# A hybrid decoder layer on one core: the first norm's factor is applied to the results instead of to x

## What is computed

```python
h = rmsnorm(x, norm1[l])           # x * rsqrt(mean(x*x) + EPS) * norm1, per token
z = h @ w_in[l]                    # D = 1024 channels in
(z_rx, z_ry, z_q, z_kc, z_vc, z_ks, z_vs, z_kw, z_vw, z_ng, z_mg) = ...
xr = rg_lru(causal_conv(z_rx, conv_w, conv_b), ...)
y_a = (xr * gelu(z_ry)) @ w_rg_out
q  = rmsnorm(z_q per head, q_norm);  k_s, k_w = rmsnorm(z_ks), rmsnorm(z_kw) per head
kc = rmsnorm(compress(z_kc, ...));   vc = compress(z_vc, ...)   # pos added, 2 layers, gelu
y_b = nsa(q, kc, vc, k_s, z_vs, k_w, z_vw, sigmoid(z_ng)) @ w_nsa_out
x = x + (sigmoid(z_mg)[0] * y_a + sigmoid(z_mg)[1] * y_b) @ w_o
# then the second norm and the SwiGLU block, which the change leaves alone
```

## Time and profile before

| what | value |
|---|---|
| time, median of 3 runs | 483.1 us (482.95 to 483.11) |
| the profiled execution | 483.16 us |
| its span, first to last instruction | 481.4 us |
| granted TensorE clock | 1.000 |
| busy: TensorE, VectorE, ScalarE, POOL | 475.2, 354.7, 280.3, 16.3 us |
| read from HBM | 83.22 MB, 175 GB/s over the span |

### The profile page before, as it was taken

How to read it: one execution, slowest core, us unless ns; L and a number is a source line. 1 busy time by engine, 2 the same in 40 slices (tenths; PEclk the granted TensorE clock), 3 DMA queues, 4 the chain that set the end, 5 groups by cost and what they waited for, 6 DMA issues and landing times.

```text
span 481.4 us, 7336 instructions
## 1 busy us (share of the span) xinstructions
PE 475.2 (99%) x2795; PEld 410.0 (85%) x2795; DVE 354.7 (74%) x630; ACT 280.3 (58%) x451; POOL 16.3 (3%) x27
## 2 busy tenths in 40 slices
PE   7999999999999999999999999999999999999997
PEld 7998998788999777877788888888888888888886
DVE  3999899699897886766754758777777777764332
ACT  4755886775777897566753435755555555453320
POOL 2000210220000000000000000000000000000000
PEclk9999999999999999999999999999999999999999
DMA  8755979724243346243434452655555455555402
GB/s 309 264 170 195 372 290 257 274 88 175 88 144 120 135 159 231 91 174 95 167 116 147 150 205 83 247 197 199 208 199 176 176 181 191 207 208 175 174 1 87
DMA packets 12993, 85.78 MB, mean 178 GB/s; under 512 B 1568, under 2 KB 1824, under 8 KB 3104
## 3 DMA queue, kind: packets, MB, share of 16 engines
q1 hardware_dynamic: 12096, 82.32, 47.5%
q0 software_dynamic: 432, 2.10, 1.5%
q10 hardware_dynamic: 432, 0.91, 0.5%
HBM read 83.22 MB, written 1.05 MB: 175 GB/s over the span
## 4 chain that ended last, share of the span: by engine, by line
PE 98%; DVE 0%; POOL 0%; issue 0%; ACT 0%; POOLq 0%; DVEq 0%
PE bank L1121 19%; PE bank L1122 19%; PE bank L1123 19%; PE bank L1159 16%; PE bank L1162 8%; PE bank L1295 3%; PE bank L1242 2%; PE bank L1331 2%; PE bank L1535 1%; PE bank L1304 1%; PE bank L1252 1%; PE bank L1379 1%; PE bank L1314 1%; PE bank L1338 1%; PE bank L1335 1%; PE bank L1279 0%
## 5 line engine op out<-in xcount | busy, mean ns | idle before, releaser
L680 DVE TENSOR_TENSOR w_lo<-raw,w_hi 128x2048 fp32r<-128x2048 f32 x71 | 162.5, 2290 | 49.9 <-ACT w_hi L375 49.6
L375 ACT ACTIVATE w_hi<-raw 128x2048 fp32r<-128x2048 f32 x72 | 138.0, 1917 | 48.0 <-PE bank L1123 41.4
L1159 PE MATMUL bank<-h_hl,w_hi 128*128 128x512 f32 x336 | 80.3, 391 | 0.0
L1159 PEld LDWEIGHTS bank<-h_hl,w_hi 128*128 128x128 f32 x336 | 61.7, 188 | 11.9
L1121 PE MATMUL bank<-w_hi,h_hl 128*128 128x512 f32 x160 | 63.6, 398 | 0.0
L1123 PE MATMUL bank<-w_hi,h_hl 128*128 128x512 f32 x160 | 62.5, 390 | 0.0
L1122 PE MATMUL bank<-w_lo,h_hl 128*128 128x512 f32 x160 | 62.4, 390 | 0.0
L1121 PE MATMUL bank<-w_hi,act 128*128 128x512 f32 x150 | 59.1, 394 | 0.0
L1123 PE MATMUL bank<-w_hi,act 128*128 128x512 f32 x150 | 58.5, 390 | 0.0
L1122 PE MATMUL bank<-w_lo,act 128*128 128x512 f32 x150 | 58.4, 390 | 0.0
L1162 PEld LDWEIGHTS bank<-h_hl,w_lo 128*128 128x128 f32 x336 | 43.1, 191 | 1.6
(11 more groups left out here) (245 smaller groups left out, 740.2 us busy)
## 6 DMA issues: line engine op xcount, KB each, us to landing
raw<-stream_dram SPq DMA_DIRECT2D x72, 1024.0 KB, 4.8
w<-stream_dram SPq DMA_DIRECT2D x4, 1024.0 KB, 9.2
raw<-stream_dram SPq DMA_DIRECT2D x2, 512.0 KB, 7.5
act<-act POOLq DMA_DIRECT2D x2, 512.0 KB, 13.0
xs<-x_dram POOLq DMA_DIRECT2D x1, 1024.0 KB, 5.2
out_dram<-xs SPq DMA_DIRECT2D x3, 256.0 KB, 2.0
xs<-x_dram ACTq DMA_DIRECT2D x1, 512.0 KB, 5.0
xs<-x_dram SPq DMA_DIRECT2D x1, 512.0 KB, 4.8
```

The source lines that it names most:

```text
L375: sc.activation(w_hi[:, i % HL, :], raw[:, i % RAW, :], ACT.Copy).then_inc(hi_ready, 1)
L680: ve.tensor_tensor(w_lo[:, i % HL, :], raw[:, i % RAW, :], f(w_hi[:, i % HL, :]), ALU.subtract).then_inc(lo_ready, 1)
L1159: ins = pe.matmul(acc(u + mt)[:, :], w_hi[:, s, c:c + P], a_hl[:, k, :, :].rearrange("p x s -> p (x s)"), start=n == 0, stop=n == 2 * KC - ...
```

## The change

**Start.** xn and its wait are gone. TensorE turns x itself as each half has landed, right after the 28 warm-up transposes; the 6 behind the wait are dropped, and the later 6 are 4 and 2. The parameters are issued ahead of x's second half. Slot 0's first half is split in two quarters, placed between the chunks of h by hand, and its second half stands behind chunk 5. VectorE multiplies the identity by the factor (diag_x), and TensorE multiplies ones by it (two products), so that psum[3] holds the factor of each token along the row on every partition; ScalarE copies this to tok_x. POOL clears one more constant (ones_x).

**Panels.** ScalarE's squares, copies and tanh take the factor (or half of it) as a scale per partition: kk, qa, qb, vv, mga, mgb, and the gates, whose tanh is now two instructions.

**Direct slots.** For each rx slot VectorE multiplies the bank by tok_x into rx_tok at the top of its turn, then gives the bank back; ScalarE's L566 and the convolution read rx_tok. For kc and vc it multiplies the bank in place ahead of the position adds. For ry, POOL copies tok_x to tok_y and multiplies B by it, slot by slot, before Gelu.

```diff
@@ POOL @@
-            pool.wait_ge(pool_chain, 4)
+            pool.memset(ones_x, 1.0).then_inc(pool_chain, 1)
+            pool.wait_ge(pool_chain, 5)
...
+            pool.wait_ge(tok_x_ready, 1)
+            pool.wait_ge(asq_used, 3)
+            pool.tensor_copy(tok_y, tok_x).then_inc(tok_moved, 1)
+            pool.wait_ge(tok_moved, 1)
+            for r in range(4):
+                u = USE_RY[r]
+                pool.wait_ge(acc_free[u % 4], u // 4 + 1)
+                pool.tensor_tensor(B[:, 2 * r:2 * r + 2, :], B[:, 2 * r:2 * r + 2, :], tok_y.unsqueeze(1).broadcast_to([P, 2, S]),
+                                   ALU.mult).then_inc(ry_scaled, 1)
@@ ScalarE @@
+            sc.dma_start(prm[:, :], params[:, :]).then_inc(prm_in, 16)
             sc.dma_start(xs[:, 1, :], x[P:2 * P, :]).then_inc(x1_in, 16)
-            sc.dma_start(prm[:, :], params[:, :]).then_inc(prm_in, 16)
...
-            sc.wait_ge(first_half, 16)
-            sc.activation(w_hi[:, 0, 0:1024], raw[:, 0, 0:1024], ACT.Copy).then_inc(hi_half, 1)
-            sc.wait_ge(landed[0], 16)
-            sc.activation(w_hi[:, 0, 1024:2048], raw[:, 0, 1024:2048], ACT.Copy).then_inc(hi_ready, 1)
...
-            chunks_hi(MISC["xT"], 0, G1)
+            chunks_hi(MISC["xT"], 0, G1, 0, 2)
+            first_quarter(0)
+            chunks_hi(MISC["xT"], 0, G1, 2, 3)
+            first_quarter(1)
+            chunks_hi(MISC["xT"], 0, G1, 3, 6)
+            sc.wait_ge(landed[0], 16)
+            sc.activation(w_hi[:, 0, 1024:2048], raw[:, 0, 1024:2048], ACT.Copy).then_inc(hi_ready, 1)
+            chunks_hi(MISC["xT"], 0, G1, 6, KC)
             split_hi(1)
+            sc.wait_ge(x_spread, 1)
+            sc.activation(tok_x, psum[3][:, 0:S], ACT.Copy).then_inc(tok_x_ready, 1)
...
-                    sc.activation(sq[:, t, :], acc(use + t)[:, :], ACT.Square).then_inc(squares, 1)
+                    sc.activation(sq[:, t, :], acc(use + t)[:, :], ACT.Square, scale=rsx[:, t:t + 1]).then_inc(squares, 1)
...
-                    acc_ready(FIRST["rx"] + r)
+                    sc.wait_ge(rx_scaled, r + 1)
@@ VectorE @@
-            for t in range(T2):
-                ve.tensor_scalar(xn[:, t, :], xs[:, t, :], rs[:, NORM_X, t:t + 1], None, ALU.mult).then_inc(xn_ready, 1)
...
+            chunks_lo(MISC["xT"], 0, G1, 0, 2)
+            ve.wait_ge(consts, 4)
+            ve.wait_ge(rs_ready, rs_count(NORM_X))
+            for t in range(T2):
+                ve.tensor_scalar(diag_x[:, t, :], ident[:, :], rsx[:, t:t + 1], None, ALU.mult).then_inc(diag_x_ready, 1)
+            first_quarter(0)
+            chunks_lo(MISC["xT"], 0, G1, 2, 3)
+            first_quarter(1)
+            chunks_lo(MISC["xT"], 0, G1, 3, 6)
...
+                r = i - FIRST["rx"] - 1
+                if 0 <= r < 4:
+                    u = USE["rx"] + r
+                    ve.wait_ge(slot_done, FIRST["rx"] + r + 1)
+                    ve.wait_ge(tok_x_ready, 1)
+                    ve.tensor_tensor(rx_tok[:, r, :].rearrange("p (m s) -> p m s", m=2), acc(u)[:, :].rearrange("p (m s) -> p m s", m=2),
+                                     tok_x.unsqueeze(1).broadcast_to([P, 2, S]), ALU.mult).then_inc(rx_scaled, 1)
+                    ve.wait_ge(rx_scaled, r + 1)
+                    ve.engine_nop().then_inc(acc_free[u % 4], 1)
...
+                        both = acc(u)[:, :].rearrange("p (m s) -> p m s", m=2)
+                        link(ve.tensor_tensor(both, both, tok_x.unsqueeze(1).broadcast_to([P, 2, S]), ALU.mult))
...
-                    ps = acc(USE["rx"] + r)
+                    ps = rx_tok[:, r, :]
...
-                    ve.wait_ge(xr_ready, r + 1)
-                    ve.engine_nop().then_inc(acc_free[(USE["rx"] + r) % 4], 1)
@@ TensorE @@
-            pe.wait_ge(rs_ready, rs_count(NORM_X))
-            keep_busy(6)
             for t in range(T2):
-                pe.wait_ge(xn_ready, t + 1)
+                pe.wait_ge((x_in, x1_in)[t], 16)
...
-            keep_busy(6)
+            keep_busy(4)
+            pe.wait_ge(diag_x_ready, 2)
+            for t in range(T2):
+                ins = pe.matmul(psum[3][:, t * P:(t + 1) * P], ones_x, diag_x[:, t, :], start=True, stop=True)
+            ins.then_inc(x_spread, 1)
+            keep_busy(2, 2)
```

More of the change, by code:

```diff
@@ L132, in hybrid_layer @@
         psum = [banks[:, b, :] for b in range(8)]
-        xn = scr[:, 0:2048].rearrange("p (t n) -> p t n", t=T2)
+        ones_x = scr[:, 0:128]
+        diag_x = scr[:, 128:384].rearrange("p (t n) -> p t n", t=T2)
+        tok_x = pbuf[:, 2048:2304]
+        tok_y = asq3[:, 0:S]
         smraw = scr[:, 5504:6144]
         xsq = scr[:, 2048:3072]
+        rx_tok = scr[:, 2048:4096].rearrange("p (r n) -> p r n", r=4)
         kz = v_sb
@@ L264, in hybrid_layer @@
         RS_BEFORE = [0, 1, 3, 5, 7, 8]
+        rsx = rs[:, NORM_X, :]
+        rsx_half = ss[:, NORM_X, 2:4]
         def rs_count(n, t=0):
@@ L411, in squares_and_copy @@
                     sc.wait_ge(sq_summed, 2 * (n - NORM_K))
+                else:
+                    sc.wait_ge(rs_ready, rs_count(NORM_X))
                 for t in range(T2):
[L413 removed]
+                    sc.activation(sq[:, t, :], acc(use + t)[:, :], ACT.Square, scale=rsx[:, t:t + 1]).then_inc(squares, 1)
                 for t in range(T2):
[L415 removed]
+                    sc.activation(dst[:, t, :], acc(use + t)[:, :], ACT.Copy,
+                                  scale=rsx[:, t:t + 1]).then_inc(acc_free[(use + t) % 4], 1)
             def q_hi(pnl):
@@ L446, in _ @@
                         u = USE["vv"] + t
-                        sc.activation(v_sb[:, t, :], acc(u)[:, :], ACT.Copy).then_inc(acc_free[u % 4], 1)
+                        sc.activation(v_sb[:, t, :], acc(u)[:, :], ACT.Copy, scale=rsx[:, t:t + 1]).then_inc(acc_free[u % 4], 1)
                     sc.wait_ge(kcT_done, 1)
@@ L514, in _ @@
                     sc.wait_ge(misc_done, misc_count(m))
-                    sc.activation(gates[:, :, :, :].rearrange("p t b h -> p (t b h)"), misc(m)[:, 0:96], ACT.Tanh,
-                                  scale=0.5).then_inc(misc_free[m % 4], 1)
+                    sc.wait_ge(rs_half, 1)
+                    for t in range(T2):
+                        ins = sc.activation(gates[:, t, :, :].rearrange("p b h -> p (b h)"), misc(m)[:, 48 * t:48 * t + 48], ACT.Tanh,
+                                            scale=rsx_half[:, t:t + 1])
+                    ins.then_inc(misc_free[m % 4], 1)
                 if i == 0:
@@ L628, in _ @@
                             dst = mtt[:, t, :] if pnl < 2 else mt1[:, t, (pnl - 2) * 512:(pnl - 1) * 512]
-                            sc.activation(dst, acc(u)[:, :], ACT.Tanh, scale=0.5).then_inc(acc_free[u % 4], 1)
+                            sc.activation(dst, acc(u)[:, :], ACT.Tanh, scale=rsx_half[:, t:t + 1]).then_inc(acc_free[u % 4], 1)
                 for v in range(2):
@@ L1262, in _ @@
                     for c in (j, j + 4):
-                        ins = pe.transpose(misc(m)[:, c // 4 * S + t * P:c // 4 * S + (t + 1) * P], xn[:, t, c * P:(c + 1) * P], ident[:, :])
+                        ins = pe.transpose(misc(m)[:, c // 4 * S + t * P:c // 4 * S + (t + 1) * P], xs[:, t, c * P:(c + 1) * P], ident[:, :])
                     if t == 1:
                         ins.then_inc(misc_done, 1)
-            keep_busy(6)
+            keep_busy(4)
+            pe.wait_ge(diag_x_ready, 2)
+            for t in range(T2):
+                ins = pe.matmul(psum[3][:, t * P:(t + 1) * P], ones_x, diag_x[:, t, :], start=True, stop=True)
+            ins.then_inc(x_spread, 1)
+            keep_busy(2, 2)
             def first_x(u):
```

39 lines of the change are left out of this document (24 added, 15 removed).

## The result

The changed kernel takes 488.73 us, median of 4 executions (487.61 to 489.49), against 483.11 us (482.95 to 483.19, 4 executions): ratio 1.0113, 95% interval 1.010 to 1.0125. Slower, as forecast, by 5.6 us instead of 4.2. The profiled execution took 488.72 us, 5.56 us more than the one of before.

A forecast was written before the change was run, and what follows sets the result against it. TensorE, busy 99% of the span, bounds the kernel; VectorE's chain is close behind. The vc block's end, 82.56 + 3.9 + 1.5 = 87.9 us, makes TensorE 4.2 us late: 483.16 + 4.2 = 487.4, median 487.3, range 485.0 to 488.8.

The forecast's parts named there:

- The start: From x's turns to VectorE's low part of slot 1: that part +0.9 us late, bounds +0.4 and +1.3.
- The four rx slots: VectorE's products ahead of the low parts, 0.73 us each, less 0.3 us: +2.6 us on its chain.
- First gap: TensorE's third rg group, waiting for ScalarE's first kk copy, starts 2.9 us later; VectorE's slot 8 low part +3.9 us.
- The clock: Rival, 8%: the rg slots' gap of some 2 us lowers the clock, 2.5 us more, 489.8 us.
- Second gap: Compressor's products wait for VectorE's vc block, ending at 87.9 us after +3.9 and +1.5: TensorE 4.2 us late.
- 83.79 less 82.56: Start of the compressor's products less end of the vc block before; slack taken as 1.1 us at L1535.
- 0.9 + 2.6 + 0.4 + 1.5 - 1.1: Lateness from start, rx products, ScalarE's scales, kc and vc products, less slack at the compressor's products.
- After that: Behind the compressor's products: no further loss; low parts, loads, gates and POOL's work have slack or lie in idle time.
- Either end is covered: POOL's copy and four products, 0.69 to 2 us each, cost nothing: last B copy 155.3 us, second Gelu 167.85 us.
- the bounds of the sum: All costs at their lower bounds give +2.6 us, 485.7; at their upper bounds +5.3 us, 488.4.
- only the start: Rival, 8%: VectorE and ScalarE make up their lateness in the rg stage; slot 0's 0.7 us stays, 483.8 us.
- the start pays: Rival, 6%: slot 0 starts 1.1 us earlier and nothing behind it is bound by VectorE, 482.0 us.

The follow-up runs named there:

- no rx products: Changed kernel without VectorE's four products on the rx slots, the bank read directly and released after the convolution; 485.06 us.
- no products at all: Changed kernel with x's second half ahead of the parameters, 20 warm-up transposes, and none of the ten products by the factor (rx, kc, vc, ry); 483.19 us.
- no ry products: Changed kernel without POOL's four products on the ry results, its waits kept; 488.63 us.
- x1 first: Changed kernel with x's second half ahead of the parameters on ScalarE's queue and 20 warm-up transposes instead of 28; 487.52 us.
- change mended: Changed kernel with x's second half first, 20 warm-up transposes, and kk squares and copies ahead of the split of xr; 488.20 us.
- copies ahead: Changed kernel with ScalarE's squares and copies of the two kk banks ahead of its split of xr for rx slot 3; 487.07 us.
- start alone: Kernel before, with ScalarE taking the second half of slot 0's high part behind the fourth chunk of h; 483.02 us.
- before plus one: Kernel before with one unused 128x512 product on VectorE, in the turn of rx slot 0; 483.44 us.
- plus four: Kernel before with four unused 128x512 products on VectorE, one ahead of each low part in the rx turns; 484.84 us.
- plus POOL: Kernel before with four unused 128x512 products on POOL, each behind the copy of a ry bank; 483.06 us.

## Why the prediction was right, and where it was off
**The start: right in kind, too large.** Turns at 8.5 us (8.29), first high part 9.86 (9.65), first product 12.4 (12.25), slot 0 late by 0.7 (0.46), VectorE's low part of slot 1 late by 0.9 (0.54, within the bounds 0.4 to 1.3). The scatter of the warm-up's end, 7.58 to 8.86 us, was not in the sum.

**The four rx slots: right.** Products of 0.684 us, 0.72 to 0.74 from start to start, 0.73 forecast. They and what goes with them made 3.49 - 0.54 = 2.95 us instead of 2.6, since 0.3 us of idle time came in ahead of the first. With the smaller start this cancelled, which is luck: 52.28 us against 52.3. The convolutions cost 2.70 us from SBUF and 2.68 from the bank. By an estimate from the figures of the Trainium skill that the prediction weighed ("VectorE: DVE Perf Modes", section "The TRN2 errata") they would have taken 2.3 us; this trace does not agree.

**First gap: right.** Forecast +2.9, measured +3.05. VectorE's low part of slot 8, released by ScalarE's high part: forecast +3.9, measured +3.83.

**The clock: left out of the sum, a rival at 8% that came true in its mechanism.** The price was 2.5 us by the start's length and the time 489.8; it was 1.55 us on TensorE, in three of four executions, and in part hidden: covering the gap gave 0.9 us.

**Second gap: the right time by an incomplete list.** The step that failed is "83.79 less 82.56" as TensorE's slack. The load of the compressor's weights had only 0.2 us. It did not show in the changed kernel, since there the load landed with the vc block; that is luck too. The vc block ended at 88.60 us instead of 87.9, the difference being the 0.7 us for which VectorE waited for ScalarE behind the slow groups:
```profile
65.00 4.51 DVE L714 TENSOR_TENSOR w_lo<-raw,w_hi 128x2048 fp32r<-128x2048 f32 x2 [0.72 <-ACT w_hi L392]
```
Changed, TensorE is 4.9 us late there, forecast 4.2 (the prediction's own terms, 0.9 + 2.6 + 0.4 + 1.5 - 1.1, give 4.3).

**After that: wrong.** "Either end is covered" looked only at who waits for POOL's products and not at whom they hold up. One of them started 0.03 us ahead of a VectorE instruction with two inputs in SBUF: 0.70 us. The Trainium skill, "SBUF — State Buffer", section "SBUF: two separate sides", says that a VectorE instruction with two SBUF inputs and a GpSimd instruction that reads SBUF use a shared pair of ports, and that whichever starts first keeps it for its whole instruction. The traces agree for VectorE: behind POOL 1.79 us, ahead of it 0.69. That the ports are the cause is the page's account; what the runs show is the longer instruction, in six traces of six, and that it goes with POOL's product.

So 4.2 forecast and 5.6 measured differ by two effects that the sum put at nothing, 0.7 us each: the clock, through ScalarE, and POOL. The slower outcome and its main cause, the length of VectorE's chain, were the forecast's. That 488.73 us lies inside the stated range, 0.07 us from its end, is luck in part: the bounds of the sum end at 488.4, only the rest of the range was left for the clock's rival, and POOL's 0.7 us stood in no part of it. The rivals "only the start" and "the start pays" fell with "no rx products" (3.67 us of the loss gone) and with "no products at all", which shows no gain even with an earlier start than the change has.

## What to carry to other kernels
Before moving work onto an engine, list every wait that ends within a microsecond of the bounding engine's arrival, loads included: a load that is issued behind that engine's results is late when it is. A gap in the densest engine can cost twice, since the clock may fall behind it; filling it with idle transposes is cheap but pays only what no other chain takes back (0.9 us of 1.55 here). A product that "nobody waits for yet" can still lengthen the instruction that runs beside it.

## What the runs showed of the hardware
The granted clock fell to 0.50 behind idle gaps of 1.9 us by the waits' account (changed kernel, "no ry products", "x1 first") and of 2.1 us ("change mended"), and stayed at 1.00 behind 2.15 us in "copies ahead". The gaps are those of the profiled executions; by the clock over the span it fell in three of four executions of the changed kernel, of "no ry products" and of "change mended", in all four of "x1 first", and in none of "copies ahead". So the length of the gap alone does not decide, and what does is not shown. The stretch at the lower level lasted 3.4 us in the changed kernel (55.3 to 58.8 us) and in "change mended" (87.0 to 90.5 us). In the changed kernel POOL's product of 128x512 took 1.28 us where VectorE's sum was held up behind it, and 1.61 to 2.91 us elsewhere. The longest part of the load of the compressor's weights took 17.3 to 18.5 us from issue to landing in five kernels that issue it alike (before, start alone, before plus one, plus four, plus POOL). A per-partition scale on ScalarE cost 0.57 us from start to start for 512 columns against 0.48 without.
